# A mixture-of-experts block: one-hot products in two halves, the first expert's gate-and-up products ahead of the table product, and SyncE waiting by pass counts

## What is computed

```python
scores = sigmoid(x @ router_w)                   # 32 experts in 4 groups of 8
grp    = the group with the largest sum of its two best (scores + router_b)
expert = the two best experts of that group      # per token, TOP_K = 2
gate   = scores of the two, divided by their sum
# every token goes to its two experts
h = silu(x @ w_gate[e]) * (x @ w_up[e])          # 1024 -> 512
y[token] += gate * (h @ w_down[e])               # 512 -> 1024
out = layer_norm(ALPHA * x + y)
```

## Time and profile before

| | |
|---|---|
| median of three runs | 1072.84 us (1071.12 to 1073.37) |
| the profiled execution | 1071.65 us, its span 1069.7 us |
| TensorE busy | 977.9 us (91% of the span) |
| VectorE, ScalarE, GpSimd busy | 474.0, 289.5, 226.3 us |
| moved by DMA | 256.68 MB |
| share of queue 1 (SyncE's loads) in the time of the 16 DMA engines | 59.0% |

### The profile page before, as it was taken

How to read it: one execution, slowest core, us unless ns; L and a number is a source line. 1 busy time by engine, 2 the same in 40 slices (tenths; PEclk the granted TensorE clock), 3 DMA queues, 4 the chain that set the end, 5 groups by cost and what they waited for, 6 DMA issues and landing times.

```text
span 1069.7 us, 17631 instructions
## 1 busy us (share of the span) xinstructions
PE 977.9 (91%) x6604; PEld 432.2 (40%) x6605; DVE 474.0 (44%) x1053; ACT 289.5 (27%) x474; POOL 226.3 (21%) x336
## 2 busy tenths in 40 slices
PE   7999999999999999899998889988888888887774
PEld 3644455455456446444444333323333333332221
DVE  0696454464464464423238333343444444443333
ACT  1114311322222143100024233333333333332321
POOL 3000010010010010033033233333333333332322
PEclk9999999999999999999999998999999999999998
DMA  9432311221211220483937999999999999999992
GB/s 284 125 80 59 79 41 42 59 61 41 60 41 42 59 59 4 157 286 131 413 139 255 382 412 416 369 417 417 414 416 414 415 415 414 415 414 415 416 405 111
DMA packets 96900, 256.68 MB, mean 240 GB/s; under 512 B 17484, under 2 KB 62540, under 8 KB 72016
## 3 DMA queue, kind: packets, MB, share of 16 engines
q1 hardware_dynamic: 85024, 240.57, 59.0%
q0 software_dynamic: 11024, 13.20, 3.6%
q10 hardware_dynamic: 800, 2.15, 0.5%
HBM read 260.66 MB, written 21.23 MB: 264 GB/s over the span
## 4 chain that ended last, share of the span: by engine, by line
PE 54%; SPq 14%; DMA 12%; DVE 8%; issue 6%; POOL 3%; ACT 2%; POOLq 1%; ACTq 0%; DVEq 0%; PEldq 0%
SPq L506 13%; PE proj L1464 13%; PE proj L1423 11%; DMA y_rows<-const,raw 6%; PE proj L1655 5%; PE bank L1644 5%; PE bank L1784 4%; PE bank L1566 4%; DMA pass_sb<-x_rows,raw 3%; DMA xT_sb<-w_gu 3%; PE bank L1805 2%; PE proj L1431 1%; PE proj L1442 1%; DVE arena L1009 1%; POOL pass_sb L578 1%
## 5 line engine op out<-in xcount | busy, mean ns | idle before, releaser
L1464 PE MATMUL proj<-xT_sb,ring 128*128 128x512 f32 x384 | 185.7, 611 | 0.0
L1784 PE MATMUL bank<-arena 128*64 128x512 f32 x544 | 122.4, 596 | 18.1 <-DMA arena<-w_gu 9.3
L1423 PE MATMUL proj<-xT_sb,ring 128*128 128x512 f32 (+1 forms) x272 | 119.1, 594 | 0.0
L1347 DVE TENSOR_TENSOR const<-bank,const 128x512 f32<-128x512 f32 x33 | 22.8, 691 | 159.0 <-DMA const<-y_rows,raw 159.0
L1464 PEld LDWEIGHTS proj<-xT_sb,ring 128*128 128x128 f32 x384 | 66.9, 189 | 63.0 <-issue 59.2
L1784 PEld LDWEIGHTS bank<-arena 128*64 128x64 f32 x544 | 42.6, 137 | 97.8 <-issue 81.9
L1423 PEld LDWEIGHTS proj<-xT_sb,ring 128*128 128x128 f32 (+1 forms) x272 | 50.8, 188 | 64.6 <-issue 64.5
L852 ACT ACTIVATE pass_sb<-bank 128x256 f32<-128x256 f32 x33 | 12.7, 385 | 197.2 <-PE bank L1784 197.2
L1784 PE MATMUL bank<-gates,arena 128*64 128x512 f32 x256 | 57.4, 596 | 7.9 <-PE bank L1805 4.1
L595 POOL DMA_INDIRECT const<-y_rows,raw x33 | 34.6, 1050 | 124.7 <-DMA y_rows<-const,raw 123.9
L544 POOL MEMSET arena<- 64x64 f32 x8 | 1.2, 145 | 276.2 <-DVE arena L1026 242.4
(11 more groups left out here) (310 smaller groups left out, 1333.6 us busy)
## 6 DMA issues: line engine op xcount, KB each, us to landing
arena<-w_gu SPq DMA_DIRECT2D x64, 1024.0 KB, 22.7
gates<-w_gu SPq DMA_DIRECT2D x32, 1024.0 KB, 22.5
arena<-w_down SPq DMA_DIRECT2D x24, 1024.0 KB, 26.8
ring<-w_in SPq DMA_DIRECT2D x42, 512.0 KB, 3.9
gates<-w_down SPq DMA_DIRECT2D x16, 1024.0 KB, 24.4
xT_sb<-w_gu SPq DMA_DIRECT2D x16, 1024.0 KB, 25.6
branches<-w_down SPq DMA_DIRECT2D x16, 1024.0 KB, 26.3
ring<-w_gu SPq DMA_DIRECT2D x16, 1024.0 KB, 24.9
```

Source lines behind the costliest of these rows:

```text
L1423: ins = pe.matmul(proj[0:w, b, :], ring[:, slot, k, 0:w], xT_sb[:, k, :], start=(k == 0), stop=(k == KT - 1))
L1464: ins = pe.matmul(proj[:, gate_at["bank"], :], ring[:, gate_at["slot"], k, :], xT_sb[:, k, :], start=(k == 0), stop=(k == KT - 1))
L1784: ins = pe.matmul(bank[SLOTS * h:SLOTS * h + SLOTS, 0, :], xeT[:, k % 4, SLOTS * (k // 4):SLOTS * (k // 4) + SLOTS], gu[k // 2][:, k % 2, ...
```

## The change

1. The ranks of the first two token tiles are counted alone (`ranks`) and signalled; VectorE makes their one-hots right then (`first_slots(0)`), and TensorE multiplies them (`first_rows`, into `proj[:, 1]`) before the second half is chosen. `s_onehot` is raised twice `s_x1st` becomes two semaphores, and chunks 0 and 1 of set 3 are loaded each after its own pair of waits (`home_of_rows`).
2. TensorE does chunks 0 to 2 of the first expert's gate and up right after the tokens' transposes, then the table product, then chunk 3, the statistics, the transposes of `h`, the down product, and only then the tokens' transposes of pass 1.
3. The ln2 rows are loaded by ScalarE's queue, after the silu of pass 0, and VectorE copies them before it copies the turned tokens of pass 1.
4. `s_used` is raised six times in every pass; VectorE writes a table `last_i` of each expert's last pass, and SyncE reads from it what to wait for. Loads of expert 4 may begin before those that wait for the table.
5. Two of five marks' fillers and three of four fillers after the first transposes are gone. The first four experts are written out on TensorE and SyncE ahead of their loops.

```diff
+            def home_of_rows(n):
+                sp.wait_ge(s_x1st[n], 32)
+                sp.wait_ge(s_onehot, n + 1)
+                load(3, n, 3)
+
+            home_of_rows(0)
             sp.wait_ge(s_x1, TT)
             load(3, 2, 3)
-            sp.wait_ge(s_x1st, 16 * TT)
-            sp.wait_ge(s_onehot, 1)
-            for c in (0, 1):
-                load(3, c, 3)
-
-            sp.wait_ge(s_tab, 1)
-            load(2, 5, 2)
-
-            sp.wait_ge(s_more, 1)
-            for i, dst in ((0, y_e), (1, x2)):
...
+            home_of_rows(1)
+
+            def last_pass(e):
+                return sp.value_load(last_i[0:1, bass.ds(e, 1)], min_val=0, max_val=PASSES - 1)
+
+            def reload(e, b, last, chunks=range(NCH)):
-                for c in range(NCH):
-                    sp.wait_ge(s_used, used + c + 2)
+                for c in chunks:
+                    sp.wait_ge(s_used, last * NCH + (c + 2))
...
+            sp.wait_ge(s_first, 1)
+            last = last_pass(0)
+            reload(SETS, 0, last, (0, 1, 2))
+
+            sp.wait_ge(s_tab, 1)
+            load(2, 5, 2)
+
+            reload(SETS, 0, last, (3, 4, 5))
+            for b in range(1, SETS):
+                reload(SETS + b, b, last_pass(b))
...
@@ scalar: one_pass
                 act.activation(warm[:, 1:2], warm[:, 0:1], ACT.Silu)
+                if first:
+                    act.wait_ge(s_more, 1)
+                    act.sem_inc(s_ye, 1)
                 act.wait_ge(s_hp, p + 1)
                 act.activation(h_e, bank[:, 0, 0:FE // 2], ACT.Silu).then_inc(s_silu, 1)
+                if first:
+                    for i, dst in ((0, y_e), (1, x2)):
+                        for h in range(2):
+                            at = 2 * SGU + 2 * D + D * i + T * h
+                            act.dma_start(dst[SLOTS * h:SLOTS * h + SLOTS, :],
...
@@ vector
             logits(2)
+            def first_slots(lo):
+                dve.wait_ge(s_rank, lo // 2 + 1)
+                for c in (lo, lo + 1):
+                    dve.tensor_scalar(first_hot[:, c, :], C("slot_iota")[:, 0:SLOTS], rank_ps[:, c, 0:1], chosen[:, c + 1, 0:1],
+                                      ALU.is_equal, MUL).then_inc(s_firsthot, 1)
+
+            first_slots(0)
             gates_part(0)
...
+            first_slots(2)
...
+            dve.tensor_tensor(last_i[:, :], count[:, INCL, :], C("iota")[:, 0:N_EXP], ADD).then_inc(s_first, 1)
...
-            products(0)
+            gated(0)
+            h_turned(0)
             dve.wait_ge(s_lnback, 64)
             dve.tensor_copy(ln2_g, y_e)
             dve.tensor_copy(ln2_b, x2).then_inc(s_gains, 1)
+            turned(1)
...
@@ tensor
             pe.wait_ge(s_chosen, 1)
-            counted(0, True, False)
+            ranks(range(0, 2), "earlier", slice(1, 3), start=True, stop=False)
+            ranks(range(1, 2), "ones", slice(1, 2), start=False, stop=True).then_inc(s_rank, 1)
+            pe.wait_ge(s_x1, 2)
+            for c in (0, 1):
+                ins = first_rows(c)
+            ins.then_inc(s_onehot, 1)
...
+            def one_pass(p, b, loads):
+                pe.wait_ge(s_yp, p + 1)
+                pe.sem_inc(s_used, 1)
+                pe.wait_ge(s_xeT, p + 1)
+                gate_up(b, loads)
+                turn(p + 1)
+                pair_stats(p)
+                h_turned(p)
+                down(p, b, loads)
...
+            gate_up(0, 16, (0, 1, 2))
+            table()
+            gate_up(0, 16, (3,))
+            pair_stats(0)
+            h_turned(0)
+            down(0, 0, 16)
+            turn(1)
+
+            pe.wait_ge(s_first, 2)
...
-                with pe.If(extra > 0):
-                    with pe.Fori(0, extra) as n:
-                        one_pass(first + n, b, loads, False)
-                one_pass(first + extra, b, loads, True)
+                if not begun:
+                    one_pass(first, b, loads)
+                with pe.If(extra > 0):
+                    with pe.Fori(0, extra) as n:
+                        one_pass(first + n + 1, b, loads)
```

More of the change, by code:

```diff
@@ L1735, in _ @@
             pe.wait_ge(s_chosen, 2)
-            counted(2, False, True).then_inc(s_rank, 1)
+            ranks(range(3, 5), "ones", slice(3, 4), start=False, stop=False)
+            ranks(range(4, 5), "ones", slice(4, 5), start=False, stop=False)
+            ranks(range(2, 4), "earlier", slice(3, 5), start=False, stop=True).then_inc(s_rank, 1)
             pe.wait_ge(s_x1, TT)
-            for c in range(TT):
-                pe.wait_ge(s_firsthot, c + 1)
-                for h in range(2):
-                    ins = pe.matmul(bank[SLOTS * h:SLOTS * h + SLOTS, 0, :], first_hot[:, c, :], x1[:, c, T * h:T * h + T],
-                                    start=(c == 0), stop=(c == TT - 1))
+            for c in (2, 3):
+                ins = first_rows(c)
             ins.then_inc(s_onehot, 1)
@@ L1795, in one_pass, with down @@
                 ins.then_inc(s_hTp, 1)
-                if last:
-                    pe.sem_inc(s_used, 1)
+                pe.sem_inc(s_used, 1)
+            def down(p, b, loads):
                 pe.wait_ge(s_hT, p + 1)
                 pe.wait_ge(s_ye, p + 1)
-                wd = [v.rearrange("p (f h n) -> p f h n", f=2, h=2) for v in w_chunk[b][4:6]]
-                for f in range(4):
-                    if f % 2 == 0:
-                        pe.wait_ge(s_w[b][4 + f // 2], loads)
-                    for h in range(2):
-                        ins = pe.matmul(bank[SLOTS * h:SLOTS * h + SLOTS, 1, :], hT[:, f % 2, SLOTS * (f // 2):SLOTS * (f // 2) + SLOTS],
-                                        wd[f // 2][:, f % 2, h, :], start=(f == 0), stop=(f == 3))
-                    if f == 1 and last:
-                        ins.then_inc(s_used, 1)
@@ L1809, in one_pass @@
-                ins.then_inc(s_yp, 1)
-            pe.wait_ge(s_first, 1)
-            pe.sem_inc(s_yp, 1)
-            def expert(e, b, loads):
+                for c in range(2):
+                    pe.wait_ge(s_w[b][4 + c], loads)
+                    w = w_chunk[b][4 + c].rearrange("p (f h n) -> p f h n", f=2, h=2)
+                    for f in range(2):
+                        for h in range(2):
+                            ins = pe.matmul(bank[SLOTS * h:SLOTS * h + SLOTS, 1, :], hT[:, f, SLOTS * c:SLOTS * c + SLOTS],
+                                            w[:, f, h, :], start=(c == 0 and f == 0), stop=(c == 1 and f == 1))
+                    ins.then_inc(s_yp if c else s_used, 1)
@@ new lines, in one_pass, with table @@
+            def one_pass(p, b, loads):
+                pe.wait_ge(s_yp, p + 1)
+                pe.sem_inc(s_used, 1)
+                pe.wait_ge(s_xeT, p + 1)
+                gate_up(b, loads)
+                turn(p + 1)
+                pair_stats(p)
+                h_turned(p)
+                down(p, b, loads)
+            def table():
+                pe.wait_ge(s_copied, 4)
+                for n in range(TOPK * TT):
+                    if n % 2 == 0:
+                        pe.wait_ge(s_hot, n // 2 + 2)
+                    for h in range(2):
+                        ins = pe.matmul(bank[SLOTS * h:SLOTS * h + SLOTS, 4, 0:3 * PASSES], slot_hot[:, n, :], pass_hot[:, n, :, :],
+                                        start=(n == 0), stop=(n == TOPK * TT - 1))
+                ins.then_inc(s_tabp, 1)
@@ L1815, in expert @@
+            turn(0, first=True)
+            keep_clock(3 * P)
+            pe.sem_inc(s_yp, 1)
+            pe.sem_inc(s_used, 1)
+            pe.wait_ge(s_xeT, 1)
+            gate_up(0, 16, (0, 1, 2))
[6 more added lines that the diff above has]
+            pe.wait_ge(s_first, 2)
+            def expert(e, b, loads, begun=False):
                 extra = pe.value_load(extra_i[0:1, bass.ds(e, 1)], min_val=0, max_val=MORE)
@@ L1825, in _ @@
+            for b in range(SETS):
+                expert(b, b, 16, begun=(b == 0))
+            with pe.Fori(1, N_EXP // SETS) as i:
                 for b in range(SETS):
```

108 lines of the change are left out of this document (40 added, 68 removed).

## The result

| | before | after |
|---|---|---|
| median | 1073.11 us (1069.44 to 1074.25) | 1076.34 us (1075.05 to 1077.16) |
| profiled execution, its span | 1071.65, 1069.7 us | 1075.68, 1073.9 us |

The ratio of after to before is 1.0039 [1.0027, 1.0051]; the two medians alone give +3.2 us (1.0030), the two profiled executions +4.0 us. Forecast were 1074.3 us and "within 0.2%, on the slow side". The time lies in the range and on the side that was named, but the change is a clear loss of twice the forecast size.

A forecast was written before the change was run, and what follows sets the result against it. The weight stream bounds the end, through one chunk release in the two-pass expert. Terms -1.3 + 2.0 + 0.8 = +1.5 us gave 1073.15 profiled, 1074.3 as median, within 0.2% on the slow side; range 1070.4 to 1077.0.

The forecast's parts named there:

- Pass 0: TensorE's first pass: gate-up from 583.1, table product 588.5 to 590.7 (1.5 us later), down 594.4 to 598.1 (5.3 us earlier).
- The turning of pass 1: Pass 1's tokens: gather issued at 592.5, landing at 599.3, turning over at 600.0; pass 1 at 600.7 without the ln2 rows.
- the landing of the ln2 rows: Ahead of VectorE's copy of pass 1's tokens: rows land 5.1 to 6.1 us after issue, at 600.7; pass 1 starts 602.7.
- The first rival: Ln2 rows land 1 to 2 us later and hold pass 1 back: +3.4 to +4.1 us, 1076.2 to 1076.9; chance 0.32.
- its three terms: Pass 1 sooner -1.3 us, clock +2.0, wait in the second pass +0.8: sum +1.5 us.
- The clock: TensorE's waits before pass 1 drop it to half clock near 602 to 606: 2.0 us lost, bounds 0 and 2.6.
- The wait in the second pass: In the two-pass expert, the second pass now waits for the down product: start 0.8 us later, bounds 0 and 0.9.
- Release plus a constant: The end is the time of the chunk release in the two-pass expert (677.65) plus a constant; earlier loads are lost.
- The fourth rival: The weight stream's start decides after all: one chunk sooner gives -2.3 us, 1070.5; chance 0.06.
- The fifth rival: TensorE's stall at 640 (2.8 us waiting, 2.6 of clock) goes: -3.9 us, 1068.9; chance 0.05.
- The first hole: Weight stream, 562 to 586 us, 7.2 us unused: earlier loads use about one chunk, 2.3 us; the second hole eats it.
- Issue time: Start of pass 1: 0.6 us allowed for the copy of the tokens until the first matmul.

The follow-up runs named there:

- held: The changed kernel, with SyncE waiting for the four ln2 row loads before issuing any chunk of expert 4: 1075.73 us, ratio 1.0034.
- rows first: Changed kernel with turned copy first, counts read early, table after two chunks, and SyncE issuing the ln2 rows ahead of expert 4's chunks: 1071.11 us, ratio 0.9993.
- the kernel with all repairs of the order: Changed kernel with turned copy first, counts read early, table after two chunks, expert 4's first chunks ahead of `home_of_rows(1)`: 1074.77 us, ratio 1.0028.
- the filled wait: The changed kernel with 24 unread matmuls around pass 1's transposes, 6 before and 18 behind: 1074.24 us, ratio 1.0026.
- turned_first: The changed kernel with VectorE's copy of pass 1's turned tokens put back ahead of the wait for the ln2 rows: 1072.39 us, ratio 1.0012.
- counts_only: The kernel before with only part 4 of the change (pass counts, `last_i`, the `s_yp` wait in `one_pass`): 1071.39 us, ratio 0.9997.
- ln2_by_sp: The changed kernel with the ln2 rows issued by SyncE after the table, ahead of chunk 3 of expert 4: 1075.72 us, ratio 1.0039.
- regs_turned: The changed kernel with the turned copy ahead of the ln2 rows and pass counts read before pass 1's transposes: 1074.52 us, ratio 1.0025.
- after_no_ln2: The changed kernel without the four ln2 row loads, the wait for them, and their use in the last norm: 1071.11 us, ratio 0.9996.

## Why the prediction was wrong

**Pass 0, right in its times.** Copy of the turned tokens at 583.25 (said: ending 583.1; it ended 583.85), table product ending at 591.2 (590.7), gather at 593.10 (592.5), down 594.91 to 598.56 (594.4 to 598.1): within 0.8 us each. For the down product this is luck: its own terms, 592.5 + 2.0 - 0.6, give 593.9 and not 594.4, and the 0.6 us were not won (592.95 to 594.91 are 2.0 us, as before).

**The turning of pass 1, missed by 1.9 us.** It was to begin at 599.3, 6.8 us after the gather's issue. Now the gather was issued at 593.10 and its tokens came after 8.1 us, 601.21. The same chunks stand in front of it: it landed in 4.6 us in `held`, in 6.1 in rows first and in 8.3 in the kernel with all repairs of the order. So the stated 600.7 for a pass 1 without the rows was too early: the kernel without them has 604.52, of which 2.3 us are issue behind the copy. Of the 6.0 us between 602.7 and 608.75 the rows make about 4.2, read from one profile each.

**The step that failed** is the landing of the ln2 rows, "They land 5.1 to 6.1 us after issue now: 600.7", with "I price at nothing for the landing". The first issue was right (593.0 for 592.9), the landing was 7.6 to 11.9 us. The earlier trace rows timed these loads where SyncE's first reload was queued behind them; the change itself puts three chunks of 1 MB and `load(2, 5, 2)` ahead of them. What stands in front decides: 3.4 to 3.8 us with nothing of expert 4 ahead and a nearly idle stream (`held`), 4.4 to 5.4 behind `load(3, 1, 3)` and `load(2, 5, 2)` (rows first), 5.1 to 6.1 in before, 7.6 to 11.9 behind five. Pass 1 started at 608.75 instead of 602.7. The first rival named this mechanism and its place, "issued with three chunks of reloads ahead", but priced it at 1 to 2 us from rows none of which had that queue. The chunks alone would not have given the size. As an estimate, at the stream's 2.53 us each, the five issued from 587.06 to 592.1 would be through at 599.7 and the sixth, issued at 594.04, at 602.2, while the last row landed near 606.8. So the runs show what makes the landing longer, not the rule by which; that stays open.

**The time inside the range: luck.** With what was measured in the places of its three terms (+4.7 for pass 1, +2.85 for the clock, +0.5 for the second pass) the prediction's sum is +8.1 us, 1080.9, above its range. Only 4.5 us reached the release, because before's long wait at 640 and its clock loss (2.79 + 2.6) were not there. The first rival's 1076.2 to 1076.9 holds the measured 1076.34 in the same way: its mechanism was right, its landing (1 to 2 us more, pass 1 at 604 to 604.7) far too small, and the stall that went made up for it.

**The clock, right in kind.** It was to fall near 602 and cost 2.0, at most 2.6 us; it fell in the first wait, near 600.9, stood at 0.50 from 602 to 614 and cost 2.85 in pass 1's gate-up and, falling again, 1.7 in pass 2's down product, where no term was. The Trainium skill (TensorE: Matmul & The Clock Gate, "Why this matters for your kernels") warns of idle gaps between bursts of matmuls; the trace agrees, and the filled wait shows that filling it pays only for the clock, not for the wait. The length of the wait just before does not tell alone, as the prediction took it to: behind 0.96 us (632.67) pass 2's down product took 5.4 for 3.7 us, and in the filled kernel one behind 0.85 us (643.46) took 5.35 for 3.65, while in `turned_first` one behind 1.60 us (644.64) lost nothing.

**The wait in the second pass, too dear.** It was put at 0.8 us; there it costs 0.5 us, and the same edit makes each ordinary pass start 0.4 us sooner, which was not seen. Alone it costs nothing (0.9997).

**Release plus a constant, right, with a limit.** 392.05 us before, 391.75 after, 391.75 to 392.65 in the seven experiments whose hole stayed. The fourth rival (the stream's start decides) became true in every kernel that closed the hole, with the span at 1068.9 to 1072.6. It was given 0.06 for the change itself, where the hole did stay, and grew as said. The two limits lie within a few us of each other in all these kernels, and none of them was clearly faster than before.

**The stall at 640, half seen.** The fifth rival had it gone with an early pass 1. It is gone in most of these kernels, with pass 1 late (after, `counts_only`) or early (rows first: 600.94, and no wait for a gather above 1.29 us up to the release). In after, the missing stall and the shorter gaps took 3.1 us off the loss: 7.6 us at the end of pass 1's gate-up, 4.5 at the release.

**The first hole, not used.** One chunk, 2.3 us, was to go there; 0.4 us did. Chunk 0 of set 3 came early (574.43), but its neighbour waited until 587.06 for the last row store, which took 8.6 us to land, priced like before's 5.2 to 6.5.

**Issue time, missing.** I put 0.6 us for the copy and the first matmul right behind it. With the reads of the pass counts behind `turn(1)` the matmul comes 2.1 to 2.3 us after the copy's end where nothing covers them; in after the longer wait for the rows hid it.

**Open.** With the turned copy first, the kernel that also reads the counts early has the higher median (1074.52 against 1072.39) though its profiled span is lower (1070.1 against 1071.8); the intervals of the two ratios overlap, [1.0013, 1.0038] and [0.9999, 1.0025]. Single runs of both spread over 7.0 and 8.5 us, and no profile shows what the longer of them waited for. Why the last row store took 8.6 us, with the DMA engines nearly idle from 585 on, was not tried apart; the chunk issued at 574.43 stands in front of it as the chunks stand in front of the ln2 rows. And part 5 was never tried alone: in five of the experiments that leave out the marks' fillers (`turned_first`, `ln2_by_sp`, `held`, `regs_turned`, `after_no_ln2`) the profile shows a granted clock of 0.50 from 570 to 574, in before and after 1.00, and pass 0's gate-up begins between 583.07 and 585.66 (after: 583.90). Times of the start of pass 1 in different profiles therefore carry a shift of 1 to 2 us that is not their edit's.

## What to carry to other kernels

When a load is moved, look at what the same change puts into the DMA queues ahead of it, and do not price its landing by where it stood before; issue small rows that an engine waits for ahead of megabyte loads that nobody waits for yet. Ask of every semaphore behind such a load which queues stand behind it: here the same rows held one queue by order and another by a semaphore, and repairing one showed the other. Find both limits of a stream, the release and its start, before moving work: here pass 1 started 7.8 us sooner at full clock in rows first, and the kernel was still level with before.

## What was not expected of the hardware

- **Landing of small rows:** the same four loads took 3.4 to 3.8 us with nothing issued beside them and 7.6 to 11.9 us behind five loads of 1 MB, issued by ScalarE both times. A gather of GpSimd shows it too: 4.6 against 8.1 us in the same two kernels. The Trainium skill (DMA: Bandwidth & Descriptors, "Issuing engines are not separate DMA queues") says that a second issuer saves only issue time; the trace agrees as to the time of the kernel (1.0039 with either issuer), though the last row landed in 8.8 us from SyncE and in 11.9 from ScalarE, each in one profile.
- **Reading registers is not free:** with the four reads of two experts' pass counts behind the transposes, TensorE stands 2.80 and 2.99 us between transposes and matmul, 2.1 and 2.3 of them after the copy that it needs is out; with the reads ahead of the transposes it stands 0.79 us, copy included.
- **A short wait can cost the clock:** the granted clock fell to 0.50 behind waits of 0.85 and 0.96 us for a gather, and stayed at 1.00 behind one of 1.60 us.
